# Six feed-forward parts with every engine's queue in a new order: block sums earlier, weight quarters loaded one by one

## What is computed

```
D_FF = 2816
# first block, layer i
h = rms_norm(x, g_ffn_pre[i]);  gu = h @ w_gate_up[i]
f = (silu(gu[..., :D_FF]) * gu[..., D_FF:]) @ w_down[i]
x = x + rms_norm(f, g_ffn_post[i])
# second block, layer l
x = x + 0.5 * swiglu(rmsnorm(x, ffn1_norm[l]), ffn1_wg[l], ffn1_wu[l], ffn1_wd[l])
...mixers...
x = x + 0.5 * swiglu(rmsnorm(x, ffn2_norm[l]), ffn2_wg[l], ffn2_wu[l], ffn2_wd[l])
```

## Time and profile before

| | |
|---|---|
| median of 3 runs | 1687.7 us (1687.43 to 1690.64) |
| profiled execution, own time | 1686.27 us |
| its span, first to last instruction | 1684.5 us |
| mean granted TensorE clock | 0.981 of full speed |
| TensorE busy (PE) | 1595.2 us, 95% |
| VectorE busy (DVE) | 1260.0 us, 75% |
| ScalarE busy (ACT) | 953.0 us, 57% |
| DMA | 161 GB/s over the span |

### The profile page before, as it was taken

How to read it: one execution, slowest core, us unless ns; L and a number is a source line. 1 busy time by engine, 2 the same in 40 slices (tenths; PEclk the granted TensorE clock), 3 DMA queues, 4 the chain that set the end, 5 groups by cost and what they waited for, 6 DMA issues and landing times.

```text
span 1684.5 us, 21355 instructions
## 1 busy us (share of the span) xinstructions
PE 1595.2 (95%) x8492; PEld 1315.4 (78%) x8492; DVE 1260.0 (75%) x1408; ACT 953.0 (57%) x1364; POOL 93.3 (6%) x184
## 2 busy tenths in 40 slices
PE   9999899999989998899999998899799999998998
PEld 8688678868867887778877887788677887787776
DVE  6868876786887777786757696867768765778686
ACT  7755555685555554555567554554546456655463
POOL 1000000120000030000020000002000002000000
PEclk9999999999999999999999999999899999999999
DMA  8237444524744566454530555447463552074532
GB/s 298 100 122 253 142 168 167 179 72 150 252 139 175 174 188 226 159 169 147 174 125 2 183 192 205 145 149 247 147 224 110 175 174 76 18 272 132 204 101 100
DMA packets 163059, 270.86 MB, mean 161 GB/s; under 512 B 4968, under 2 KB 98400, under 8 KB 162960
## 3 DMA queue, kind: packets, MB, share of 16 engines
q1 hardware_dynamic: 159984, 261.87, 45.6%
q0 software_dynamic: 2544, 7.09, 1.6%
q10 hardware_dynamic: 432, 0.53, 0.1%
HBM read 268.42 MB, written 1.05 MB: 160 GB/s over the span
## 4 chain that ended last, share of the span: by engine, by line
PE 54%; DVE 22%; DMA 11%; ACT 8%; issue 3%; SPq 1%; POOL 0%; DVEq 0%; POOLq 0%; ACTq 0%
DVE w_lo L1546 9%; DMA raw<-in_ffn_wd 7%; PE bank L2501 6%; PE bank L2502 6%; PE bank L2503 6%; PE bank L2595 6%; DVE fold_raw L1704 4%; PE pair L2625 4%; ACT w_hi L975 3%; PE pair L2706 3%; PE pair L2708 3%; DMA raw<-in_w_down 3%; PE pair L2711 3%; PE bank L2568 3%; PE pair L2629 2%
## 5 line engine op out<-in xcount | busy, mean ns | idle before, releaser
L1546 DVE TENSOR_TENSOR w_lo<-raw,w_hi 128x2048 fp32r<-128x2048 f32 x203 | 461.5, 2276 | 148.4 <-ACT w_hi L975 147.5
L975 ACT ACTIVATE w_hi<-raw 128x2048 fp32r<-128x2048 f32 (+1 forms) x207 | 392.8, 1902 | 124.0 <-DMA raw<-in_ffn_wd 59.5
L2625 PE MATMUL pair<-xt,w_hi 128*128 128x512 f32 x1296 | 312.9, 392 | 0.1
L2625 PEld LDWEIGHTS pair<-xt,w_hi 128*128 128x128 f32 x1296 | 239.0, 188 | 47.5 <-issue 0.5
L2501 PE MATMUL bank<-w_hi,hid_hi 128*128 128x512 f32 x528 | 211.4, 400 | 23.1 <-DVE w_lo L1546 23.0
L2502 PE MATMUL bank<-w_hi,hid_lo 128*128 128x512 f32 x528 | 208.0, 394 | 0.0
L2503 PE MATMUL bank<-w_lo,hid_hi 128*128 128x512 f32 x528 | 207.7, 393 | 0.0
L1546 DVE TENSOR_TENSOR w_lo<-fold_raw,w_hi 128x2048 fp32r<-128x2048 f32 x72 | 164.5, 2287 | 42.0 <-ACT w_hi L975 42.0
L2629 PEld LDWEIGHTS pair<-xt,w_lo 128*128 128x128 f32 x1296 | 167.3, 191 | 7.1
L2629 PE MATMUL pair<-xt,w_lo 128*128 128x256 f32 x1296 | 169.4, 283 | 0.0
L975 ACT ACTIVATE w_hi<-fold_raw 128x2048 fp32r<-128x2048 f32 x72 | 137.4, 1910 | 55.8 <-PE bank L2503 31.3
(11 more groups left out here) (352 smaller groups left out, 2541.9 us busy)
## 6 DMA issues: line engine op xcount, KB each, us to landing
raw<-in_ffn_wd SPq DMA_DIRECT2D x44, 1024.0 KB, 4.9
raw<-in_w_gate_up SPq DMA_DIRECT2D x28, 1024.0 KB, 5.3
raw<-in_ffn_wg SPq DMA_DIRECT2D x28, 1024.0 KB, 5.7
raw<-in_ffn_wu SPq DMA_DIRECT2D x28, 1024.0 KB, 5.4
raw<-in_w_down SPq DMA_DIRECT2D x22, 1024.0 KB, 4.8
raw<-in_w_in SPq DMA_DIRECT2D x21, 1024.0 KB, 5.2
fold_raw<-in_w_gate_up SPq DMA_DIRECT2D x16, 1024.0 KB, 10.3
fold_raw<-in_ffn_wg SPq DMA_DIRECT2D x16, 1024.0 KB, 9.9
```

The source lines that it names most:

```text
L975: act.activation(w_hi[u % RING][:, 0:filled(u)], raw_of(u)[:, 0:filled(u)], ACT.Copy)\
L1546: dve.tensor_tensor(w_lo[s][:, 0:filled(u)], raw_of(u)[:, 0:filled(u)], w_hi[s][:, 0:filled(u)].bitcast(F32), ALU.subtract)\
L2625: pe.matmul(out[:, 512 * m:512 * (m + 1)], w[0][:, c, P * m:P * (m + 1)], xt[:, 2 * SEQ * c:2 * SEQ * (c + 1)], start=(c == 0), stop=False)
```

## The change

The work is the same: the same units, the same matmuls in the same order on TensorE, the same number of instructions on VectorE, ScalarE and SyncE. What changes is the order of the queues of VectorE, ScalarE and SyncE in each of the six FFNs, and the waits that this order needs. One counting semaphore of the fold (fold_made, fold_copied, fold_gate, fold_rows) becomes one per result, since the results no longer come in one fixed sequence. Copies out of PSUM now wait by name for the reader of what they overwrite (gates_read, products_read). The load of each quarter waits only for its own tile to be free. Cut to its core, the diff is:

```
-FOLD_FIRST = (10, 25)
+FOLD_AT = ((10, 11, 12, 14, 15, 16, 17), (25, 26, 27, 29, 30, 31, 32))
...
-            def load_set(u0, k, wg, wu):
-                if k == 0:
-                    sp.wait_ge(unit_used, u0)
-                else:
-                    sp.wait_ge(lo_ready, u0 + FOLD_FIRST[k - 1] + 8)
-                first = 256 * FOLD_GROUPS[k]
-                load_fold(LEFT, quarter(wg, 0, first))
-                load_fold(UPPER, quarter(wu, 0, first))
-                load_fold(LOWER, quarter(wg, 1, first))
-                load_fold(RIGHT, quarter(wu, 1, first))
+                def fold_free(k, place):
+                    if k:
+                        sp.wait_ge(lo_ready, u + FOLD_AT[k - 1][place] + 1)
+                    else:
+                        sp.wait_ge(unit_used, u)
+                def load_left(k):
+                    fold_free(k, 3)
+                    if k:
+                        sp.wait_ge(fold_made[FOUR_SUM], fold_index(f, k))
+                    load_quarter(LEFT, quarter(wg, 0, 256 * FOLD_GROUPS[k][0]))
...
                 load_down(0)
+                load_right(0)
                 load_gate(2)
+                load_lower(0)
                 load_up(2)
-                load_set(u, 0, wg, wu)
                 load_down(1)
                 load_gate(3)
+                load_left(0)
+                load_upper(0)
                 load_up(3)
...
-                load_set(u, 1, wg, wu)
                 load_down(4)
+                load_left(1)
                 load_down(5)
                 load_gate(7)
+                load_upper(1)
                 load_up(7)
+                load_right(1)
+                load_lower(1)
```

On VectorE, the fold of groups 4 and 5:

```
-                    split_lo(v)
-                    gates(g)
-                    three_sum(k)
-                    split_lo(v + 1)
-                    four_sum(k)
-                    split_lo(v + 2)
-                    add_up(g)
-                    multiply(g)
+                upper_sum(0)
+                right_sum(0)
+                split_lo(u0 + UP_AT[3])
+                add_up(2)
+                split_lo(u0 + FOLD_AT[0][0])
+                add_cross(3)
+                multiply(2)
+                three_sum(0)
+                hidden_rest(2)
+                scale_gates(3)
+                split_lo(u0 + FOLD_AT[0][1])
+                add_up(3)
+                split_lo(u0 + FOLD_AT[0][2])
+                split_lo(u0 + DOWN_AT[2])
+                multiply(3)
+                split_lo(u0 + FOLD_AT[0][3])
+                four_sum(0)
```

On ScalarE, the same place:

```
+                quarter_rounded(0, 0)
+                gate_cross_out(3)
+                hidden_rounded(2)
+                quarter_rounded(0, 1)
+                up_cross_out(3)
+                sum_rounded(0, 2)
+                down_rounded(2)
+                sum_rounded(0, 3)
+                silu(3)
```

More of the change, by code:

```diff
@@ L43 @@
 NP = len(PLAIN_GROUPS)
+GATE_AT = {0: 0, 1: 2, 2: 5, 3: 8, 6: 20, 7: 23, 10: 35}
+UP_AT = {0: 1, 1: 3, 2: 6, 3: 9, 6: 19, 7: 24, 10: 34}
+DOWN_AT = {0: 4, 1: 7, 2: 13, 3: 18, 4: 21, 5: 22, 6: 28, 7: 33, 8: 36, 9: 37, 10: 38}
+AFTER_FOLD = {6: 0, 10: 1}
+BEFORE_FOLD = {0: 3, 1: 7}
+SLOT_FREED = {6: 4, 10: 8}
+FOLD_NAMES = {f"fold {k}": k for k in range(FOLDS)}
+SLOT_BEFORE = {0: None, 1: None, 2: 0, 3: 1, 6: 'fold 0', 7: 'fold 0', 10: 'fold 1'}
+FOLD_BEFORE = ((2, 3), (6, 7))
 LEFT, UPPER, LOWER, RIGHT = range(4)
-FOLD_TILE = {0: LEFT, 1: LOWER, 4: LEFT, 5: RIGHT, 6: UPPER, 7: LOWER}
-FOLD_SUM = {2: 1, 6: 2, 4: 3, 7: 4}
+UPPER_SUM, RIGHT_SUM, THREE_SUM, FOUR_SUM = range(4)
+FOLD_TILE = {0: LEFT, 1: LOWER, 3: LEFT, 4: RIGHT, 5: UPPER, 6: LOWER}
+FOLD_SUM = {2: UPPER_SUM, 3: THREE_SUM, 5: RIGHT_SUM, 6: FOUR_SUM}
 EPS = 1e-6
@@ L1806, in ffn @@
+                row_factors_out()
+                add_up(0)
                 scale_gates(0)
-                group(0)
-                split_lo(u0 + 4)
-                gates(1)
-                split_lo(u0 + 5)
-                group(1)
+                split_lo(u0 + UP_AT[1])
+                multiply(0)
+                split_lo(u0 + DOWN_AT[0])
+                hidden_rest(0)
                 whole_rows()
-                split_lo(u0 + 6)
+                split_lo(u0 + GATE_AT[2])
+                add_cross(1)
@@ L1814, in ffn @@
+                scale_gates(1)
+                add_up(1)
                 row_sums()
-                split_lo(u0 + 7)
-                gates(2)
-                split_lo(u0 + 8)
-                group(2)
+                split_lo(u0 + UP_AT[2])
+                multiply(1)
+                split_lo(u0 + DOWN_AT[1])
                 row_sums_rest()
+                hidden_rest(1)
+                add_cross(2)
+                scale_gates(2)
+                split_lo(u0 + GATE_AT[3])
                 upper_sum(0)
-                split_lo(u0 + 9)
@@ new lines, in ffn @@
+                split_lo(u0 + FOLD_AT[0][0])
[11 more added lines that the diff above has]
+                four_sum(0)
+                hidden_rest(3)
+                first_gate(0)
@@ new lines, in ffn @@
+                fold_rest(0, 1)
+                add_up(6)
+                split_lo(u0 + DOWN_AT[5])
+                add_cross(6)
+                split_lo(u0 + GATE_AT[7])
+                scale_gates(6)
+                multiply(6)
+                upper_sum(1)
+                split_lo(u0 + UP_AT[7])
+                hidden_rest(6)
+                split_lo(u0 + FOLD_AT[1][0])
+                three_sum(1)
+                add_cross(7)
+                scale_gates(7)
+                split_lo(u0 + FOLD_AT[1][1])
@@ new lines, in ffn @@
+                right_sum(1)
+                add_up(7)
+                split_lo(u0 + FOLD_AT[1][2])
+                split_lo(u0 + DOWN_AT[6])
+                four_sum(1)
+                split_lo(u0 + FOLD_AT[1][3])
+                split_lo(u0 + FOLD_AT[1][4])
+                multiply(7)
+                first_gate(1)
+                split_lo(u0 + FOLD_AT[1][5])
+                hidden_rest(7)
+                split_lo(u0 + FOLD_AT[1][6])
+                first_up(1)
+                split_lo(u0 + DOWN_AT[7])
@@ L2705, in product @@
                         w = w_hi[s][:, 512 * c:512 * (c + 1)]
-                        pe.matmul(out, hi[c], w, start=not more and c == 0, stop=False,
-                                  skip_group_check=more)
+                        pe.matmul(out, hi[c], w, start=not more and c == 0, stop=False, skip_group_check=more)
                         pe.matmul(out, lo[c], w, start=False, stop=False, skip_group_check=more)
@@ new lines, in product, with first_product @@
+                        last = pe.matmul(out, hi[c], w_lo[s][:, 512 * c:512 * (c + 1)], start=False, stop=(c == 3),
+                                         skip_group_check=more)
+                    last.then_inc(unit_used, 1)
+                def first_product(k):
+                    if k in BEFORE_FOLD:
+                        pe.wait_ge(gate_summed, base + PLAIN[BEFORE_FOLD[k]] + 1)
+                    else:
+                        pe.wait_ge(hidden_lo, hidden_base + FOLD_GROUPS[k - 1][1] + 1)
+                    product(k, 0, bank[0], rows_part(0, 0))
```

476 lines of the change are left out of this document (281 added, 195 removed).

## The result

| | before | after |
|---|---|---|
| median | 1687.57 us (1687.18 to 1690.64, 4 runs) | 1592.84 us (1592.59 to 1593.92, 4 runs) |
| profiled execution, its span | 1684.5 us | 1590.8 us |
| mean granted TensorE clock | 0.981 | 0.996 |

The ratio is 0.9436, with a 95% interval from 0.942 to 0.9452: 5.6% faster, 94.7 us. The forecast was 1585, the range 1578 to 1612.

What follows compares the result with a forecast made beforehand. TensorE was taken to be held by waits for VectorE at two folds per FFN and by late DMA weights in openings: 89 + 16.6 - 2 x 2 = 102 us off 1686.3 gives 1584, median 1585; range 1578 to 1612.

Steps and rivals of the forecast that it cites:

- The floor of the folds: Stretches from gate(3) to down(8): 117.3 us each without waits, 704 for six against 792.77, so 89 us lost.
- The walk of the first fold: VectorE's new queue from gate(3): add_up(3) done at 171.4, 2.7 us before the fifth product wants it; remainders at 173.6, 175.8.
- The thin margins: Both folds: everything ready in time, by as little as 0.4 us at down(7), 0.6 at gate(6), 1.2 at gate(10).
- The rival that the stalls come back in the folds: Some waits return in the folds, 27 us if one of 4.4 us in each FFN: 1611 us; 20%.
- What was left in the openings: From gate(1) to gate(3) of FFN 2 and 4: 2 us each still lost of 16.6 together, bounds 0 and 6.
- The signs named for the openings: Openings of FFN 2 and 4 take 34 to 37 us; ScalarE's longest DMA wait there is under 6 us.
- The part on down(1): Opening of FFN 2: down(1)'s weights land by 642.1, it is ready at 646 to 649, waiting 0.6 to 3.6 us.
- the weighed rule: DMA descriptors go in ring order, so RIGHT ahead delays gate(2)'s load by 4.1 us: 1.6 us of wait, total 1587.
- with every loss gone: Whole kernel with no loss left in folds or openings: 1580 us.
- The openings keep their loss: gate(2)'s load is late instead of down(1)'s: 8 us in each of FFN 2 and 4, 1592 to 1600 us; 12%.
- The stalls only move: ScalarE's rounding behind the free slot makes later units wait instead; time stays near 1687 us, within 0.2%; 4%.
- Slower: Late LEFT or UPPER holds VectorE at upper_sum and right_sum ahead of up(3)'s remainder, delaying the fold: up to 1705 us; 4%.

Runs made afterwards that it cites:

- experiment 6: Changed kernel with four_sum and the fifth product's remainder put back ahead of add_up(3), in the first fold alone: 1613.95 us, ratio 0.9554.
- experiment 7: Changed kernel with VectorE making the remainder of down(7) twice, 2.3 us more in each FFN: 1610.8 us, ratio 0.9535.
- experiment 4: Changed kernel's VectorE and ScalarE queues, with SyncE's loads in the old order, quarters four by four: 1631.63 us, ratio 0.9672.
- experiment 1: Changed kernel with RIGHT loaded behind gate(2) and LOWER behind up(2), both still ahead of down(1): 1591.71 us, ratio 0.9425.
- experiment 3: Changed kernel with the RIGHT and LOWER loads moved behind UPPER and up(3), so no quarter is ahead of down(1): 1580.91 us, ratio 0.9366.
- experiment 2: Changed kernel with GpSimd's mixer parameter loads in FFN 2 and FFN 4 held back until gate(3) is multiplied: 1579.79 us, ratio 0.936.

## Why the prediction held, step by step

**The floor of the folds: right.** The sum of units gave 117.3 us a stretch and 89 us to gain; the windows show 117.17 and 89.8. Experiments 6 and 7 show the mechanism: one pair of steps put back, or one subtraction more, and the waits return where the walk has its margins.

**The walk of the first fold: right.** It had add_up(3) done at 171.4 and the two remainders behind it at 173.6 and 175.8. The timeline of VectorE in FFN 0 of after:

```profile
171.12 0.69 DVE L1759 TENSOR_TENSOR up_sum<-pair,up_sum 128x512 f32<-128x512 f32 x1
171.72 4.51 DVE L1646 TENSOR_TENSOR w_lo<-raw,w_hi 128x2048 fp32r<-128x2048 f32 x2
```

171.8 and 176.2: late by 0.4 us, which is how much later gate(3) started (157.88 instead of 157.5), and in time. Putting add_up back (experiment 6) brings the wait back at that place in all six.

**The thin margins: right.** No wait stands before down(7), gate(6) or gate(10); experiment 7 measures the 0.4 us at down(7), and in experiment 4 gate(6) waits in every FFN once down(4) is loaded late. The rival that the stalls come back in the folds (20%) did not happen with this order; with 2.3 us more on VectorE it does, in experiment 7.

**What was left in the openings: the term that was mis-sized.** The prediction took 2 us in each of FFN 2 and FFN 4, between bounds of 0 and 6. It is 6.2 us in each, past the upper bound and together 8.4 us more than was taken, and that, with 0.8 us more from the folds than the 89, is the 7.8 us between 1585 and 1592.84. The signs named for the openings failed too: they take 39.5 and 39.6 us instead of 34 to 37, and ScalarE's longest wait for the DMA there is 10.89 us instead of under 6.

The part on down(1) was sized well: its rounding begins at 614.57, 25.4 us after gate(1), where the landing was forecast at 24.7 (642.1 - 617.38). It was gate(2) that went wrong. Its load took 17.3 us from issue to landing, against 11.3 in the kernel before: 6.0 us more, where the forecast had 4.1. It was also issued 0.9 us later, counted from gate(1). Its remainder and add_cross(1) were done 21.3 us after gate(1) instead of 18.4, and the wait was 4.43 us instead of 1.6. The half-clock stretch behind it, 1.7 us, stood in the upper bound but not in the 2 us.

I chose the value "because DMA has less to carry between 612 and 632". The engines had no such room: from 583 to 606 us they were busy throughout, and 2.20 of the 6.11 MB were GpSimd's. The kernel before had the mark of it: in the window at 258 GB/s GpSimd's queue moved 0.99 of the 1.55 MB. I used the low rate for the weighed rule and the high one for down(1), and did not ask what made it low.

**The sums.** The losses taken off, 101.6 us, give 1586 for the median rather than 1585, and with every loss gone 1582 rather than 1580. The 1587 of the weighed rule isn't the sum of its parts: 1.6 and 3.6 us in both openings leave 95.2 us of gain, 1592.5. That this is the time measured is luck, for down(1) had no wait; one wait of 4.43 us and its half clock did it.

**The range.** 1592.84 lies outside the forecast of 1580 to 1590 (60%) and inside 1578 to 1612. The range was that wide mostly for stalls coming back in the folds, which did not come.

**The weighed rule: its direction holds, and it isn't the cause of the loss.** With RIGHT ahead, gate(2) waits 4.43 us, and with gate(2) ahead it doesn't (experiment 1). By this the trace agrees with what the Trainium skill says of descriptors consumed in ring order (DMA: Bandwidth & Descriptors, "Queues, rings and completion order"). But obeying it saved nothing (1591.71 against 1592.84 us), since down(1) then waits 4.63 us for the same stream. It took fewer bytes ahead of both (experiment 3), or nobody else on the DMA engines (experiment 2).

**"VectorE's busy time stays at 1260 us": wrong as a number, without effect.** It is 1252.1, though the instructions are as many (1408) and as long (the remainders from raw 2288 ns on average before, 2287 after). Busy time counts records that overlap once, and back to back a subtraction shown with 2.28 us is followed 2.21 us later; with fewer gaps in the queue more of them overlap, which I take to be the 8 us. In the stretches it is 97.24 instead of 105.59. Part of that is a shift: LEFT and UPPER's sums now start before gate(3), and the opening windows hold 30 to 33 us of VectorE instead of 26 to 27.

**The 1580 "with every loss gone": right as a number.** Experiments 2 and 3 measured 1579.79 and 1580.91 us.

**The rivals.** "The openings keep their loss" with 1592 to 1600, by gate(2) instead of down(1), names mechanism and time; it had 12%. It overstated what is left (8 us in each; it is 6.2). "The stalls only move", by ScalarE's rounding behind the free slot, did not happen: the stretches came down to 117.17 us. "Slower" had its condition, quarters late at upper_sum, nowhere: VectorE has no wait for the DMA in after.

## What to carry to other kernels

Walk the queue of the busiest helper engine step by step with measured durations, and read the margins: a stall here was a matter of order, and 2.3 us of the same work in each FFN cost 16 to 18 us at one place and next to nothing three units on. Where one engine's order and the loads both stand ahead of a unit, test them together, since each alone gave a part (9 and 55 us of 94.7). When a transfer is late, look for what else moves bytes in that window, other engines' small loads too, before sorting the loads of one queue.

## What the runs showed of the hardware that was not expected

- With the 2.20 MB of parameters that GpSimd loads, all DMA together moves 270 GB/s instead of 335, with the DMA engines busy in both cases, and SyncE's queue gets 3.91 MB through in 23 us instead of 7.52 (experiment 2). With the load order of after this costs 13 us in FFN 2 and FFN 4 together; with fewer bytes ahead it costs nothing that could be measured (experiment 3).
- Under that load the issues of up(2) and down(1) on SyncE last 2.12 and 7.95 us (timeline of FFN 2 of after); the same two last 0.37 us each in experiment 2. What is behind them in SyncE's queue starts late as well. GpSimd's loads aren't needed for it: in experiment 3 an issue at 610.84, after they have landed, lasts 5.28 us.
- Waits of TensorE of one length, 1.88 us, are followed by 3.25 us at about half clock in two parts and by full clock in two others (experiment 6). What tells these apart the runs don't show; it stays open. In a sum, a wait of about 2 us is worth its own length and 0.15 to 0.3 us (it is counted from a modelled end), and in six of the twelve cases of experiments 6 and 7 another 1.5 to 1.7 us.
